# Two-layer hybrid backbone: latent rows with tokens on partitions behind layer 1's output projection, router logits from column groups, squares ahead of row copies in the dense layer

## What is computed

```python
for i in range(DEPTH):                     # layer 0 dense, layer 1 experts
    sh1, sc1, gt1, sh2, sc2, gt2 = split(silu(c) @ w_mod[i] + b_mod[i], 6)
    p = split_proj(modulate(rmsnorm(x, g_mix_pre[i]), sh1, sc1) @ w_in[i])
    ...
    y_x = concatenate([gla_output(...), short_conv(...)]) @ w_out[i]
    x = x + gt1 * rmsnorm(y_x, g_mix_post[i])
    h = modulate(rmsnorm(x, g_ffn_pre[i]), sh2, sc2)
    x = x + gt2 * rmsnorm(ffn(h), g_ffn_post[i])

def moe_swiglu(h, w_r, w1e, w3e, w2e):     # 8 experts, top 2, softmax over the two
    logits = h @ w_r
    ...
```

## Time and profile before

| | |
|---|---|
| median of 3 runs | 1726.31 us (1725.66 to 1730.38) |
| profiled execution | 1724.4 us, of which the span from first to last instruction is 1722.6 us |
| mean granted TensorE clock | 0.993 of full speed |
| PE busy | 1630.1 us (95%) |
| DVE busy | 940.2 us (55%) |
| ACT busy | 528.6 us (31%) |
| read from HBM | 473.58 MB |

### The profile page before, as it was taken

The page is one execution under the profiler, slowest core; times in us unless marked ns, Lnnn a source line. Parts: engine busy times, 40 slices in busy tenths (PEclk is TensorE's granted clock), DMA queues, the critical chain, the costliest instruction groups (busy, mean ns, idle before and its releaser), DMA issues.

```text
span 1722.6 us, 21510 instructions
## 1 busy us (share of the span) xinstructions
PE 1630.1 (95%) x8580; PEld 1119.1 (65%) x8580; DVE 940.2 (55%) x1318; ACT 528.6 (31%) x667; POOL 4.0 (0%) x13
## 2 busy tenths in 40 slices
PE   6999999999999999998999999999999999988886
PEld 4688675888888885797878833788348873422222
DVE  6688765544446775699589810898118971100002
ACT  5421334200000005414577601675017740000001
POOL 0000000000000000000000000000000000000000
PEclk9999999999999999999999999999999999999999
DMA  9420976233321326328689999999999999999996
GB/s 337 164 98 1 343 253 227 70 94 95 95 97 37 134 83 213 106 91 294 270 296 370 400 366 420 419 419 421 385 419 420 420 421 416 421 419 420 420 418 267
DMA packets 132571, 476.26 MB, mean 276 GB/s; under 512 B 10626, under 2 KB 41828, under 8 KB 101732
## 3 DMA queue, kind: packets, MB, share of 16 engines
q1 hardware_dynamic: 130640, 474.25, 70.8%
q10 hardware_dynamic: 1812, 0.41, 0.1%
HBM read 473.58 MB, written 1.05 MB: 276 GB/s over the span
## 4 chain that ended last, share of the span: by engine, by line
PE 75%; SPq 9%; DVE 6%; DMA 3%; ACT 3%; issue 3%; ACTq 0%; DVEq 0%; POOL 0%; POOLq 0%
PE ps L949 10%; PE ps L951 10%; PE ps L950 10%; PE ps L1304 8%; PE ps L1419 7%; SPq L816 7%; PE ps L1411 6%; PE ps L1413 6%; PE ps L1354 3%; SPq L820 3%; PE ps L913 2%; PE ps L872 2%; DMA ring<-in_e_w 2%; DMA work<-in_e_w 2%; PE ps L1280 1%
## 5 line engine op out<-in xcount | busy, mean ns | idle before, releaser
L1304 PE MATMUL ps<-ring,work 128*64 128x512 f32 (+1 forms) x1088 | 218.5, 544 | 19.8 <-DMA ring<-in_e_w 17.0
L949 PE MATMUL ps<-ring_rounded 128*128 128x512 f32 (+1 forms) x536 | 190.5, 355 | 2.9 <-DVE norms L2431 1.6
L1304 PEld LDWEIGHTS ps<-ring,work 128*64 128x64 f32 x1088 | 74.4, 136 | 161.0 <-issue 111.5
L2061 DVE TENSOR_TENSOR ring_rounded<-ring,hT_rounded 128x2048 fp32r<-128x2048 f32 (+1 forms) x80 | 165.4, 2086 | 21.1 <-ACT hT_rounded L1943 20.5
L2650 DVE TENSOR_TENSOR norms<-work,ps 128x512 f32<-128x512 f32 (+1 forms) x20 | 11.5, 617 | 282.8 <-PE ps L1304 282.8
L951 PE MATMUL ps<-ring_rounded 128*128 128x512 f32 (+1 forms) x472 | 163.3, 346 | 0.0
L1943 ACT CAST hT_rounded<-ring 128x2048 fp32r<-128x2048 f32 (+1 forms) x80 | 139.5, 1755 | 35.2 <-PE ps L1413 27.8
L951 PE MATMUL ps<-mixT_rounded,ring_rounded 128*128 128x512 f32 x328 | 127.6, 389 | 0.0
L1354 PE MATMUL ps<-ring,mixT 128*64 128x512 f32 x480 | 110.7, 598 | 11.1 <-DMA ring<-in_e_w 11.1
L949 PE MATMUL ps<-mixT_rounded,work_rounded 128*128 128x512 f32 x304 | 118.3, 389 | 0.0
L950 PE MATMUL ps<-hT_rounded,work_rounded 128*128 128x512 f32 x304 | 118.3, 389 | 0.0
(11 more groups left out here) (318 smaller groups left out, 2797.9 us busy)
## 6 DMA issues: line engine op xcount, KB each, us to landing
ring<-in_e_w SPq DMA_DIRECT2D x204, 1024.0 KB, 17.9
ring<-in_e_w SPq DMA_DIRECT2D x112, 768.0 KB, 13.3
ring<-in_w_mod SPq DMA_DIRECT2D x20, 2048.0 KB, 9.7
ring<-in_w_in SPq DMA_DIRECT2D x11, 2048.0 KB, 8.0
ring<-in_w SPq DMA_DIRECT2D x22, 1024.0 KB, 7.9
mixT<-in_e_w SPq DMA_DIRECT2D x18, 1024.0 KB, 20.4
work<-in_e_w SPq DMA_DIRECT2D x18, 1024.0 KB, 20.8
ring<-in_w_mod SPq DMA_DIRECT2D x8, 1024.0 KB, 11.7
```

The source lines that it names most:

```text
L949: pe.matmul(acc, w_high_, x_high_, start=first, stop=False)
L1304: ins = pe.matmul(narrow_bank(w, b)[H * side:H * side + H, 0:n], xsel[:, k, 0:H], words[:, o:o + n], start=(k == 0), stop=(k == KD - 1), s ...
L2061: return dve.tensor_tensor(dst, src, high, ALU.subtract)
```

## The change

1. Layer 0, behind the output projection: of the chunks (1,1) to (1,3), the columns of (1,2) and (1,3) and the row copies of (1,2) and (1,3) move behind the squares, the normalisation and the first three dense tiles. ACT squares before it copies.
2. End of the dense layer: DVE adds seven squares of the branch where it added four, so PE makes two matmuls for the sum where it made five. Chunk (1,5)'s row copy and columns move behind layer 1's squares, the row copy of (1,6) behind the modulation, its columns behind the `q` and `k` tiles. ACT gates tiles 4 and 5 before the inverse and 6 and 7 behind the copy of row (1,4).
3. During layer 1's output projection PE transposes the residual to token rows (`xa`, sixteen transposes), which ACT copies to `htok`. DVE scales the router's weights and builds two pick matrices ahead of the branch's squares.
4. Behind it, the branch's sum of squares is taken by token (matmuls of one column). Router products of residual (`lx`) and branch (`lb`) are made with the scaled weights in four column groups, the branch is transposed (`xb`) and added to `htok` by DVE, ACT squares the token rows. Then come the rows of the gate chunks, and `lg` adds the groups. `add_branch`, eight squares, `normalise`, `modulate`, the diagonals and the transposes of `hT` go.
5. `htok` now holds the residual, not the normalised input: `select` carries the token's inverse, and `take_gather` applies scale and shift to the gathered words, tile by tile. The gate is picked as rows by one matmul for each half (`gate_row`), with bias and gain loaded as rows by two ACT loads during layer 1. `arrange` is cut in four and goes into expert 0's loop. The residual's transposes at the end (`out`) go.
6. SP's twelfth place waits for `gate` 0. The other places wait as before; chunks (1,10) and (1,11) are used behind `lb`.

```diff
 MODS = {"start": ((0, 0), (0, 1), (0, 2), (0, 3)), "keys": ((0, 4), (0, 5)), "added": ((0, 6), (0, 7)),
-        "states": ((0, 8), (0, 9)), "outputs": ((0, 10), (0, 11), (1, 0)), "residual": ((1, 1), (1, 2)),
-        "entry": ((1, 3),), "second": ((1, 4), (1, 5)), "entry1": ((1, 6),), "keys1": ((1, 7), (1, 8)),
-        "states1": ((1, 9),), "last": ((1, 10), (1, 11))}
+        "states": ((0, 8), (0, 9)), "outputs": ((0, 10), (0, 11), (1, 0)), "keys1": ((1, 7), (1, 8)),
+        "states1": ((1, 9),)}
+GATES = ((1, 10), (1, 11))
...
+            for i in range(3):
+                use(("xa", i), 4 + i)
         for m in range(KD):
             use(("y", L, m), rot(), ("wo", L, m // 4))
-        use(("yss", 2 * L), 4)
+            if L and m == 2:
+                use(("xa", 3), 7)
+        use(("yss", 2 * L), rot() if L else 4)
...
+    use(("lx",), rot())
+    for i in (0, 2, 1, 3):
+        use(("xb", i), 4 + i)
+    use(("lb",), rot())
+    for ch in GATES:
+        use(("mrow", *ch), rot(), ("mod", *ch))
+    use(("lg",), rot())
+    use(("gate", 0), rot())
     use(("pos",), 7)
-    for i in range(4):
-        use(("out", i), (0, 1, 4, 5)[i])
+    use(("gate", 1), rot())
...
-                        wait_tile(sp, ("mcol", 1, 11) if s == ESLOTS - 3 else ("y", 1, KD - 1))
+                        wait_tile(sp, ("gate", 0) if s == ESLOTS - 3 else ("y", 1, KD - 1))
...
+            def residual_rows(i):
+
+                acc = begin(("xa", i))
+                for j in range(4):
+                    o = CTX + (i // 2) * P
+                    ins = pe.transpose(acc[:, j * P:(j + 1) * P], xT[:, 4 * (i % 2) + j, o:o + P], ident[:])
+                end(ins)
+
+            def branch_rows(half):
+
+                accs = [begin(("xb", 2 * t + half), t) for t in range(TT)]
+                for j in range(4):
+                    m = 4 * half + j
+                    wait_drained(pe, ("y", 1, m))
+                    for t in range(TT):
+                        o = CTX + t * P
+                        ins = pe.transpose(accs[t][:, j * P:(j + 1) * P], hT[:, m, o:o + P], ident[:])
+                        if j == 3:
+                            end(ins)
...
-                    square_sum(("ssq", 2 * L), KD, TOK)
-                    mods("entry1")
+                    square_sum(("ssq", 2), KD, TOK)
+                    mod_cols(1, 5)
+                    mod_rows(1, 6)
...
+                    accs.append(begin(("y", L, m), m + 3 * L))
                     y_products(accs[m], m, range(0, 4))
+                if L:
+                    for i in range(3):
+                        residual_rows(i)
                 for m in range(3):
                     end(y_products(accs[m], m, range(4, KD)))
+                if L:
+                    residual_rows(3)
                 for m in range(3, KD):
                     end(y_products(begin(("y", L, m)), m, range(KD)))
-                last_square(("yss", 2 * L), n)
-                mods("residual" if L == 0 else "last")
-                square_sum(("ssq", 2 * L + 1), KD, n)
                 if L == 0:
-                    mods("entry")
+                    last_square(("yss", 0), n)
+                    mod_rows(1, 1)
+                    mod_rows(1, 2)
+                    mod_cols(1, 1)
+                    square_sum(("ssq", 1), KD, n)
+                    mod_cols(1, 2)
+                    mod_rows(1, 3)
...
+                    mod_cols(1, 3)
...
-                    added_squares(("yss", 1), 4, TOK)
-                    mods("second")
-
-
-
-            pe.wait_ge(gate_diag_ready, 1)
-            for i in range(2):
+                    last_square(("yss", 1), TOK)
+                    mod_rows(1, 4)
+                    mod_rows(1, 5)
+                    mod_cols(1, 4)
...
+            acc = begin(("yss", 2))
+            pe.wait_ge(sq_used, squares_used["yss", 2] + KD - 1)
+            for t in range(TT):
+                pe.matmul(acc[:, t:t + 1], tmp[:, 0, t * P:(t + 1) * P], ones[:, 0:1], start=(t == 0), stop=False,
+                          skip_group_check=True)
+            nsq[0] += KD
+            pe.wait_ge(sq_ready, nsq[0])
+            for t in range(TT):
+                ins = pe.matmul(acc[:, t:t + 1], sq[:, (nsq[0] - 1) % 2, t * P:(t + 1) * P], ones[:, 0:1], start=False,
+                                stop=True, skip_group_check=True)
+            end(ins)
...
+            def router_rows(name, words):
+
+                acc = begin(name)
+                for kk in range(2):
+                    for g in range(4):
+                        k = 4 * kk + g
+                        ins = pe.matmul(acc[32 * g:32 * g + 32, 0:SEQ], wr_scaled[:, k, :], words[:, k, CTX:],
+                                        start=(kk == 0), stop=(kk == 1), skip_group_check=True)
+                end(ins)
+
+            pe.wait_ge(router_scaled, 2)
+            router_rows(("lx",), xT)
+            branch_rows(0)
+            branch_rows(1)
+            router_rows(("lb",), hT)
+            for ch in GATES:
+                mod_rows(*ch)
+
+            pe.wait_ge(row_pick_ready, 1)
+            acc = begin(("lg",))
+            pe.matmul(acc[:, 2 * TT * NE:(2 * TT + 1) * NE], ones[:], wr_shift[:, 0, :], start=True, stop=True,
+                      skip_group_check=True)
+            for side, name in enumerate(("lx", "lb")):
+                wait_drained(pe, (name,))
+                for t in range(TT):
+                    at_ = (side * TT + t) * NE
+                    ins = pe.matmul(acc[:, at_:at_ + NE], router_words[:, side, t * P:(t + 1) * P], group_pick,
+                                    start=False, stop=True, skip_group_check=True)
+            end(ins)
+
+            def gate_row(i):
+
                 acc = begin(("gate", i))
-                for j in range(4):
-                    ins = pe.matmul(acc[:, j * P:(j + 1) * P], ones[:], gate_diag[:, 4 * i + j, :], start=True,
-                                    stop=True)
-                end(ins)
-
-            acc = begin(("lg",))
-            for k in range(KD):
-                pe.wait_ge(h_ready, 3 * KD + k + 1)
-                for t in range(TT):
-                    ins = pe.matmul(acc[:, t * NE:(t + 1) * NE], hT[:, k, CTX + t * P:CTX + (t + 1) * P], wr[:, k, :],
-                                    start=(k == 0 and t == 0), stop=(k == KD - 1), skip_group_check=True)
-            end(ins)
-            for i in range(4):
-                acc = begin(("ht", i))
-                for j in range(4):
-                    k = 4 * (i % 2) + j
-                    o = CTX + (i // 2) * P
-                    ins = pe.transpose(acc[:, j * P:(j + 1) * P], hT[:, k, o:o + P], ident[:])
-                end(ins)
-
+                wait_drained(pe, ("mrow", *GATES[i]))
+                end(pe.matmul(acc[:], row_pick, mrow_last if i else mrow, start=True, stop=True))
+
+            gate_row(0)
...
+            gate_row(1)
+            def wait_banks(*banks):
+
+                for b in banks:
+                    pe.wait_ge(drained[b], max(nth_of[n] for n in tile_at if bank_of[n] == b) + 1)
+
+            wait_banks(4, 5, 7)
...
+                    if L or m < KD - 1:
                         gated(("y", L, m), m, L, 2, c0)
-                inverse_rms(("yss", 2 * L), n, D)
-                gated(("y", L, KD - 1), KD - 1, L, 2, c0)
-                take_rows(*MODS["residual" if L == 0 else "last"])
-                for k in range(KD):
-                    act.wait_ge(res_ready, 2 * L * KD + k + 1)
-                    square(xT[:, k, c0:], n)
-                inverse_rms(("ssq", 2 * L + 1), n, D)
+                    if L and m == 2:
+                        take_residual(3)
                 if L == 0:
-                    take_rows(*MODS["entry"])
-                modulate(2 * L + 1, L, 3, c0, x_high if L == 0 else None)
-                if L == 0:
+                    inverse_rms(("yss", 0), n, D)
+                    gated(("y", 0, KD - 1), KD - 1, 0, 2, c0)
+                    take_rows((1, 1))
+                    for k in range(KD):
+                        act.wait_ge(res_ready, k + 1)
+                        square(xT[:, k, :], n)
+                    take_rows((1, 2))
+                    inverse_rms(("ssq", 1), n, D)
+                    modulate(1, 0, 3, 0, x_high)
+                    take_rows((1, 3))
...
+            act.activation(branch_rms, branch_rms, ACT.Exp, scale=-0.5).then_inc(branch_rms_ready, 1)
+            wait_tile(act, ("lx",))
+            drains(act.copy(router_words[:, 0, :], bank(("lx",))[:, 0:SEQ]), ("lx",))
+            for half in range(2):
+                for t in range(TT):
+                    i = 2 * t + half
+                    wait_drained(act, ("xb", i))
+                    act.activation(norms[:, i, :], htok[:, t, half * 512:(half + 1) * 512], ACT.Square,
+                                   accum_out=token_norms[:, i:i + 1]).then_inc(row_squares, 1)
```

(60 more changed lines are left out.)

284 lines of the change are left out of this document (170 added, 114 removed).

## The result

The changed kernel took 1711.78 us (median of 6 runs, 1709.34 to 1714.76), the kernel before 1725.49 in the same comparison: a ratio of 0.992 with a 95% interval from 0.9903 to 0.9937, 13.7 us less. The forecast was 1712.5. The total came out right, but partly by luck: less was won ahead of the experts than the sum said, and a gain that the sum did not have made up for it.

A forecast was written before the change was run, and what follows sets the result against it. It took the start of expert 0, plus a fixed stage, to set the end; -0.8 - 5.0 + 1.0 - 9.0 = -13.8 us took the profiled 1724.4 to 1710.6, and 1.9 for the median gave 1712.5, range 1707 to 1721.

The forecast's parts named there:

- What bounds the kernel: Whole kernel: the end is when expert 0 starts to free places, plus a stage of unchanged length.
- SP's slack: SP's queue before expert 0: places could be released as late as 878, some 35 us later, without moving the end.
- Layer 0, -0.8: Layer 0's second modulation: sum of squares ends 0.45 us earlier, row copy no longer ahead (0.35).
- End of the dense layer, -5.65 to the modulation: Layer 1's modulation: squares end 5.3 us earlier, row copy gone (0.35); about -2.5 for part 2 if squares stay slow.
- Columns of (1,6) and transposes of the residual, +0.65 and +1.0: Layer 1 on PE: columns ahead of `a` give 0.65 us back; sixteen transposes, half covered, cost 1.0 (0 to 3.65).
- Routing up to the logits, -8.2: Routing stage: logits reduced 11.0 us behind tile `y` 7 instead of 19.2.
- From the logits to the expert, -0.75: Routing's end: `pos` no longer held by the `hT` transposes, -0.9 us; `take_gather` in smaller copies, +0.15.
- the first rival, the clock: Routing stage: narrow matmuls and transposes run at 1.2 GHz throughout, about 8 us back, 1720.5; chance 0.18.
- `arrange`, 0: Expert 0 on DVE: four pieces, 3.7 us together, fit into DVE's idle time and cost nothing.
- The stage from expert 0 on, unchanged: First expert matmul to last landing: stays 838.9 us; wrong if longer by more than 2 us.
- a first expert matmul later than 860: Start of expert 0 on PE: forecast at 854.2; later than 860 would show the prediction wrong.
- sign of 674 for layer 1's modulation: Profile after, layer 1: modulation expected at 674, 5.8 us earlier.

The follow-up runs named there:

- e3: Changed kernel with the rows of the two gate chunks moved behind `lg`; median 1708.49 us, ratio to the kernel before 0.9895.
- e4: Changed kernel with four extra matmuls of 256 columns on PE ahead of gate row 0, filling its wait; median 1710.31 us.
- e5: Changed kernel with `arrange` whole again ahead of `take_gather`, out of expert 0's loop; first expert matmul 2.5 us and last landing 1.9 us later than in e2.
- e7: Changed kernel with the end of the dense layer in the order of before; first expert matmul 3.8 us and last landing 3.2 us later.
- e6: Changed kernel with SP's fifth place held until the place counts (`pos`); last landing at 1399.2 us behind layer 0's second modulation, against 1399.4 in e2.
- e1: The kernel before, unedited, profiled a second time; 1722.98 us in one execution.
- e8: The kernel before with 40 more transposes of the identity on PE at the start; 1726.38 us in one execution.
- e9: The kernel before with 20 more transposes of the identity on PE at the start; 1722.20 us in one execution.
- e10: Changed kernel with 20 more transposes of the identity on PE at the start; first expert matmul to last landing 839.9 us.
- e2: The changed kernel, unedited, run and profiled again; median 1712.84 us, ratio to the kernel before 0.9917.
- e11: Changed kernel with 40 more transposes of the identity on PE at the start; first expert matmul to last landing 835.5 us.

## Why the prediction was right, by its own steps

**What bounds the kernel: right.** The end follows the start of expert 0. The four runs that move that start for a known reason moved the landing with it, within 0.6 us: -4.7 and -4.6 (e3), -1.9 and -2.2 (e4), +2.5 and +1.9 (e5), +3.8 and +3.2 (e7). Of SP's slack, 9.4 us were there (e6).

**Layer 0, -0.8: mis-sized.** The modulation begins 15.4 instead of 15.6 us behind the branch sum, -0.2. DVE's additions pace the squares, and the last square and PE's last matmul end the sum 2.1 us behind DVE's last addition, in before as after, where I had 1.6; only part of the row copy was won.

**End of the dense layer, -5.65 to the modulation: mis-sized.** -4.4 between the first two profiles, -3.0 between the second two; e7's -4.5 has the lower clock in it, as the first pair has. PE's two matmuls of the branch sum waited 1.06 for the seventh added square, which I had put earlier, and the sum of squares ended 2.1 us behind DVE's last addition instead of 1.6. The rest is before's own clock, 0.86 and 0.80 in its first profile and 1.00 in its second. With the +0.65 behind it, -3.0 is close to the -2.5 that the prediction had as its other bound.

**Columns of (1,6) and transposes of the residual, +0.65 and +1.0: right.** From the modulation to `y` 7 it takes 158.8 instead of 157.2, +1.65.

**Routing up to the logits, -8.2: the new stage right, the old one too long by chance.** 11.4 us behind `y` 7 where I had 11.0. The 19.2 of before stands in its first profile alone: e1, e8 and e9 all have 18.0, so the gain is -6.6. The 19.2 held `lg` at the lower clock, 5.15 us where e1 took 3.96.

**From the logits to the expert, -0.75: wrong sign.** +1.1 between the first profiles. The place counts began 0.8 sooner behind the reduction, as forecast, and took 0.8 longer; from the gather's start to `take_gather` it took 0.3 longer, `select` 0.1. This is the first rival, the clock, from 849 to 859 and not throughout the stage; it did not show in 833 to 846, where the prediction had looked for it. `take_gather` cost +0.68 instead of +0.15: four tensor_scalars from PSUM took 1.37, 0.34 each, not the 0.21 of the row between SBUF tensors that I had preferred. Here the rule of the Trainium skill ("VectorE: DVE Perf Modes", section "The TRN2 errata") against cutting operations was nearer with its 1.03, and still low.

**`arrange`, 0: right** to 0.6 us (e5).

**The stage from expert 0 on, unchanged: wrong.** It became 3.2 us shorter. In before PE waited 4.6 us at a jump, so that the next expert's pieces were used up later and the transfers paused in 1200 to 1230 (370 GB/s, 373 in e1 and 367 in e10, where the changed kernel has 420 and e8 418). The changed kernel's code lies where that wait does not occur, and 20 transposes more at its start bring it back (e10). This is the term that the sum had as nothing without having looked at it.

So ahead of the experts 9.6 us were won between the first profiles and 7.6 between the second, where the sum had 13.8; 3.2 more came from the place of the code. One of the prediction's own signs of being wrong came true: it named a first expert matmul later than 860, and that came at 861.98. Of this, 3.57 are the late start-up; 858.4 remains, 4.2 later than the 854.2 of the sum. That the total fits within 1 us is luck: this loss and the unforeseen 3.2 nearly cancel. (Its sign of 674 for layer 1's modulation didn't follow from the sum either: -0.8 and -5.65 give 673.4.)

Over the four profiles of each kernel (two as it is, two with its code shifted), the first expert matmul is 7.3 us earlier on average (571.4 and 564.1), to which 0.2 from layer 0 is to be added. Where neither has a long wait in the expert stage (e8 against the changed kernel, e2 and e11), the last landing is 5.1 to 5.8 earlier; where both have it (before and e1 against e10), 5.8 to 7.8. So at like waits the change shows about half of the 13.7 up to the last landing.

Of the 13.7 between the medians the two pairs of profiles show 12.7 and 10.8 up to the last landing, and up to 0.6 behind it. The rest, up to 3 us, stays open: the profiled executions of before were faster than its median, those of the changed kernel slower than its own.

## What to carry to other kernels

Work moved behind a stage's last common input still has to be ordered within the stage: the gate rows, which the logits do not need, stood ahead of the five matmuls that the expert waits for, and moving them was worth 4.6 us more. A gap on PE ahead of narrow matmuls was paid twice here, as the wait and as the lower clock of what followed, so it is worth trying to put independent work into it. In a long program an edit of any kind shifts the code, and up to 5 us of the expert stage here came and went with that (835.0 to 839.9): shift both versions by a few instructions before a small gain is put down to the edit. And take a second profile of the kernel before: one profile's dip of the clock stood in this sum as if it were the kernel's own.

## What the runs showed of the hardware that was not expected

A wait that no engine, semaphore or transfer of data in the profile explains stood at one jump, 4.61, 4.86 and 5.22 us in three of the thirteen profiles, and was gone or elsewhere in kernels that differ only in where the code lies. It also occurs without a jump: 2.29 us (e8) and 1.47 us (e11) in a run of 128 matmuls of 64x128, one every 33 ns. All such waits of over 1 us ended 2.4 to 2.7 us behind the start of a 16 KB transfer of the instruction queue.

Adding 1.97 us of matmuls to PE made the kernel 2.5 us faster by the medians (1710.31 against 1712.84). Of this, the profiles show 2.2 at the last landing.
